# Every block its own leg, with scores, selection and attention as wide as its causal keys

## The chip, the cores and the metric

The kernel is one program on one NeuronCore of a Trainium2 chip. The metric is the device time of one execution in microseconds; the times shown are from three executions, and one more execution was profiled.

## What is computed

Two layers over 512 positions of width 1024. Each layer normalises its input, projects it once, and runs three mixers beside each other: a state-space group, a gMLP group and a sparse attention group with eight heads. Their outputs go through one output projection and are added to the input. Then follows the PEER part: each position picks 128 experts (8 heads of 16), and each expert is one row of 1024 numbers in the table peer_u and one in peer_v. The attention and the PEER part, cut to what matters here:

```python
topk = min(256, L // 4)                      # 128
key_chunk = jnp.arange(L) // CHUNK           # chunks of 64
...
    score = jnp.einsum('bth,bths->bts', wi, jax.nn.relu(s))
    adm = key_chunk[None, :] <= (qpos // CHUNK)[:, None]
    score = jnp.where(adm[None], score, -jnp.inf)
    sel_score, sel = lax.top_k(score, topk)
    valid = jnp.isfinite(sel_score)
    ...
    logits = logits - slopes[None, None, :, None] * dist[:, :, None, :]
    logits = jnp.where(valid[:, :, None, :], logits, -jnp.inf)
    probs = jax.nn.softmax(logits, axis=-1)
...
    act = jax.nn.gelu(jnp.einsum('tkd,td->tk', peer_u[e], hx))
    return jnp.einsum('tk,tkd->td', g * act, peer_v[e])
```

A query sees the keys of its own 64-position chunk and of those before it. Of a block of 128 queries, block b sees at most (b + 1) * 128 keys, and those of block 0 see at most 128, which is as many as the selection takes.

## The kernel before

The 512 positions are four blocks of 128. The program is a row of ten **legs**, and it is a software pipeline: leg (l, b) runs the mixers and the routing of block b in layer l, and beside them the PEER work of blocks before it. These go one leg behind (the dots with peer_u) and two legs behind (the mixing of peer_v). I write (0,0) to (1,3) for the eight legs with mixers; two tail legs without mixers follow. Leg (0,0) has no gathers at all, (0,1) has those of peer_u alone, and all later ones up to the first tail leg have both. The helper `legs` (L163) lists them, and legs 2 and 3 of each layer stand in the program once, as the body of a loop (`eng.Fori(2, NB)`).

The gathers: `fetch_u` and `fetch_v` on GpSimd (POOL, L231 and L238) each bring 128 rows, one per partition, 512 KB together, into one of the eight buffers of ringU or ringV. GpSimd works in program order: four U fetches, then four V fetches, 32 times a leg. Before a U fetch it waits until VectorE has made the dot that used the buffer (`S["dots"]`), before a V fetch until TensorE has mixed the buffer (`S["mixed"]`). A dot is one instruction on VectorE over 128x1024 (L709). A mixing step is 16 listed matmuls on TensorE over four buffers (L430), and 32 steps make a leg.

The order is written out by hand. VectorE and TensorE both run in program order, and the tables DOTS and MIX say how many dots (of 128) and mixing steps (of 32) are done by each stage of the mixers; DOTS_FIRST and MIX_FIRST hold for block 0 of a layer:

```python
"scored": 38, "picked": [38 + (r + 1) * 10 // 16 for r in range(16)],
"heads": [48 + (h + 1) * 26 // 8 for h in range(8)], "values": 82
...
"gated": 7, "picked": 11, "heads": [11, 12, 13, 13, 14, 15, 16, 17]
```

The attention part of a leg, by engine. TensorE makes the scores of four index heads (L578, into pw). ScalarE (ACT) takes their relu (L347). VectorE weighs and adds them (L1028, L1031), adds the mask `am`, and takes the top 128 in 16 rounds of MAX and MATCH_REPLACE over 512 columns (L1037, L1038), with dots between the rounds; what was replaced is the selection, and L1040 and L1041 make the penalty `D_` of it. Beside that TensorE makes mixing steps, and in block 0 of a layer also the last three of twelve modulation products (L461), and then the logits of the first two heads (L602).

For each head h then: VectorE adds `D_` to the logits (L1058) and takes the maximum (L1061); ScalarE takes the exponential (L372); VectorE scales the head before by the reciprocal sum (L1050, L1052), and makes three or four dots. TensorE transposes the probabilities in four pieces of 128 (L438), ScalarE copies them (L299), TensorE multiplies them with the cached keys in four pieces (L616), makes the logits of head h + 2, and where the table says so one mixing step. After the eighth head come the value projection (L627), the output projection (L636), the second norm, and the queries and routing. The next leg begins when all engines have met (`meet`, L155 on).

SyncE (SP) loads the weights through two buffers, in program order; in block 0 of a layer the load of norm2_g (L1251) waits for the first sum of the scores, `S["scored"]`.

## Time and profile before

| | |
|---|---|
| median of 3 runs | 3995.33 us (3994.73 to 3996.36) |
| the profiled execution | 3987.24 us, of it the span 3985.4 us |
| busy: VectorE, GpSimd, TensorE, ScalarE | 2473.5, 2298.0, 1942.4, 240.0 us |
| DMA | 1282.43 MB, 322 GB/s over the span |
| of the 16 DMA engines' span | 71.4% fetches of GpSimd, 13.7% the other large queue |

The span is the time from the first to the last instruction. The profiled execution is 8 us, or 0.2%, under the median of the three runs. An engine's busy time says how long it computed, not whether anyone waited for it: for that the timeline of a leg has to be read, with what ended each wait in brackets.

### The profile page before, as it was taken

How to read it: one execution, taken by the hardware profiler on the slowest of the kernel's cores; microseconds unless marked ns; L12 is line 12 of the kernel's file. 1: busy time of each engine (PE TensorE's matmuls, PEld its weight loads, DVE VectorE, ACT ScalarE, POOL GpSimd, SP SyncE). 2: the span in 40 equal slices, each digit the busy share in tenths (PEclk: the TensorE clock that was granted, in tenths of full speed). 3: DMA queues.
4: the chain of work that ended last, by engine and by line, in shares of the span. 5: the costliest groups of instructions: out<-in, count | busy, mean ns of one | idle time of the engine just before them, and what ended most of it. 6: DMA issues, size and time to landing. Idle time of an engine off the chain costs nothing. (4 is left out here: it accounts for less than half of the span.)

```text
span 3985.4 us, 30915 instructions
## 1 busy us (share of the span) xinstructions
PE 1942.4 (49%) x10338; PEld 984.3 (25%) x10338; DVE 2473.5 (62%) x5939; ACT 240.0 (6%) x539; POOL 2298.0 (58%) x2063
## 2 busy tenths in 40 slices
PE   7762351646344552676735363545526462233344
PEld 3542331413122220243314131322204130000000
DVE  4527878774768557567577746785577748544300
ACT  0110010001000100000100010001000000000000
POOL 0002455665767576456656657675766666777654
PEclk9876665767667675887767676666757685666667
DMA  7424777988989798999989889897989898999987
GB/s 236 140 75 154 236 251 256 346 342 325 408 308 390 281 402 313 333 410 378 350 306 368 343 320 399 318 395 273 402 311 373 297 373 350 368 409 409 350 303 272
DMA packets 417266, 1282.43 MB, mean 322 GB/s; under 512 B 52810, under 2 KB 63818, under 8 KB 417106
## 3 DMA queue, kind: packets, MB, share of 16 engines
q0 software_dynamic: 294912, 1073.87, 71.4%
q1 hardware_dynamic: 103252, 202.59, 13.7%
q10 hardware_dynamic: 18944, 3.96, 0.5%
q8 instruction: 87, 1.43, 0.1%
q14 instruction: 71, 0.58, 0.0%
HBM read 1271.89 MB, written 8.39 MB: 321 GB/s over the span
## 5 line engine op out<-in xcount | busy, mean ns | idle before, releaser
L709 DVE CUSTOM_DVE_ANT_0 ringU<-ringU,h2g 128x1024 f32<-128x1024 f32 x1024 | 1222.8, 1223 | 731.2 <-DMA ringU<-in_peer_u,idx_g 661.6
L238 POOL DMA_INDIRECT ringV<-in_peer_v,idxT x960 | 1050.7, 1094 | 731.0 <-PE py L430 469.4
L231 POOL DMA_INDIRECT ringU<-in_peer_u,idx_g x960 | 1101.6, 1147 | 499.4 <-issue 275.8
L430 PE MATMUL py<-ringV,wm 128*32 128x512 f32 x4096 | 771.2, 893 | 1071.4 <-DMA ringV<-in_peer_v,idxT 857.0
L430 PEld LDWEIGHTS py<-ringV,wm 128*32 128x32 f32 x4096 | 152.2, 143 | 1567.2 <-issue 1512.3
L496 PE MATMUL pj<-hT,wring 128*128 128x128 f32 (+1 forms) x2560 | 330.2, 295 | 51.2 <-DMA wring<-in_w_in 44.4
L496 PEld LDWEIGHTS pj<-hT,wring 128*128 128x128 f32 (+1 forms) x2560 | 321.0, 205 | 81.6 <-DMA wring<-in_w_in 53.6
L231 POOL DMA_INDIRECT ringU<-in_peer_u,idx_w x64 | 67.2, 1050 | 386.2 <-DVE gate_w L1156 357.6
L438 PE MATMUL pj<-ident,wk 128*128 128x128 f32 x264 | 63.3, 378 | 426.5 <-DVE wk L1052 365.4
L461 PE MATMUL pj<-wring,mixT 128*128 128x512 f32 x288 | 140.4, 644 | 70.8 <-DMA wring<-in_w_mod 66.7
L1175 DVE TENSOR_TENSOR wk<-py,g2g 128x1024 f32<-128x1024 f32 x8 | 9.8, 1224 | 265.6 <-PE py L430 263.7
L438 PEld LDWEIGHTS pj<-ident,wk 128*128 128x128 f32 x264 | 39.5, 185 | 495.2 <-DVE wk L1052 430.0
L616 PE MATMUL pw<-hT,ckv_all 128*128 128x128 f32 x512 | 121.6, 412 | 43.9 <-ACT hT L299 43.9
L616 PEld LDWEIGHTS pw<-hT,ckv_all 128*128 128x128 f32 x512 | 103.8, 301 | 65.9 <-ACT hT L299 65.9
L1058 DVE SCALAR_TENSOR_TENSOR wk<-wk,pw 128x512 f32<-128x512 f32 x64 | 43.8, 684 | 119.6 <-PE pw L602 119.3
L636 PE MATMUL pj<-wring,mixT 128*128 128x512 f32 x256 | 115.6, 610 | 1.4 <-ACT mixT L299 1.4
L238 POOL DMA_INDIRECT ringV<-in_peer_v,idxTn x64 | 74.6, 1165 | 51.5 <-PE py L430 34.4
L461 PEld LDWEIGHTS pj<-wring,mixT 128*128 128x128 f32 x288 | 57.9, 207 | 150.9 <-issue 123.3
L1037 DVE MAX8 top<-wk 128x8 f32<-128x512 f32 x128 | 88.6, 692 | 2.1
L438 PE MATMUL pj<-ident,hh 128*128 128x128 f32 x128 | 31.4, 427 | 119.6 <-DVE hh L926 119.6
L372 ACT ACTIVATE wk<-wk,cols 128x512 f32<-128x512 f32 x64 | 46.2, 722 | 704.8 <-DVE cols L1061 704.8
L1038 DVE MATCH_REPLACE8 wk<-top,wk 128x512 f32<-128x512 f32 x128 | 86.5, 675 | 0.0
(295 smaller groups left out, 2206.7 us busy)
## 6 DMA issues: line engine op xcount, KB each, us to landing
wring<-in_w_in SPq DMA_DIRECT2D x28, 2048.0 KB, 20.1
wring<-in_w_mod SPq DMA_DIRECT2D x24, 2048.0 KB, 10.1
wring<-in_w_out SPq DMA_DIRECT2D x16, 2048.0 KB, 20.3
wring<-in_peer_w_q SPq DMA_DIRECT2D x16, 2048.0 KB, 21.9
ringU<-in_peer_u,idx_g POOLq DMA_INDIRECT x960, 7.9
ringV<-in_peer_v,idxT POOLq DMA_INDIRECT x960, 7.3
wring<-in_w_in SPq DMA_DIRECT2D x8, 784.0 KB, 17.3
x_mix<-xs SPq DMA_DIRECT2D x8, 512.0 KB, 19.2
```

The costliest lines, as they stand in the source:

```text
L231: pool.indirect_dma_start(out=ringU[k % NR][:, :], out_offset=None, in_=ux, in_offset=bass.IndirectOffsetOnAxis(ap=idx[:, k:k + 1], axis=0 ...
L238: pool.indirect_dma_start(out=ringV[r % NR][:, :], out_offset=None, in_=vx, in_offset=bass.IndirectOffsetOnAxis(ap=idx[:, 32 * j + m:32 * ...
L372: a.activation(wk[:, 3072 + (h % 2) * 512:3584 + (h % 2) * 512], wk[:, 2048 + (h % 2) * 512:2560 + (h % 2) * 512], ACT.Exp, bias=col(NM + ...
L430: mm = t.matmul(py[32 * j:32 * j + 32, c * 512:(c + 1) * 512], wm[e % 2][:, at:at + 32], ringV[(4 * m + j) % NR][:, c * 512:(c + 1) * 512] ...
L438: m = t.transpose(dst, src, ident[:, :])
L461: t.matmul(pj[n % 2][:, :], crep[:, k * 128:(k + 1) * 128], wt[:, k * 512:(k + 1) * 512], start=k == 0, stop=False)
L496: mm = t.matmul(dst, wt[:, k * gc + c0:k * gc + c0 + width], hT[:, k * 128:(k + 1) * 128], start=k == 0, stop=k == KT - 1)
L616: mm = t.matmul(pw[:, 1024 + (h % 4) * 128:1152 + (h % 4) * 128], ckv_all[:, s * 128:(s + 1) * 128], hT[:, (h % 2) * 512 + s * 128:(h % 2) ...
L636: mm = t.matmul(pj[n][:, :], mixT[:, k * 128:(k + 1) * 128], wt[:, k * 512:(k + 1) * 512], start=k == 0, stop=k == KT - 1)
L709: v.tensor_tensor_reduce(out=ringU[k % NR][:, :], in0=ringU[k % NR][:, :], in1=h2g[:, :], scale=1.0, scalar=0.0, op0=ALU.mult, op1=ALU.add ...
L1037: link(v.max(top8[:, :], sc))
L1038: link(v.match_replace(sc, top8[:, :], sc, GONE))
```

## The change

It does four things. The loops are written out, so that b is a number in every leg. `seen(b)` gives W = (b + 1) * 128, and scores, relus, the sums, the selection's rounds, the eight heads' logits, maxima, exponentials and scalings are W columns wide in place of 512; transposes and products with the keys have b + 1 pieces in place of four. In block 0 the scores, relus, sums and all 16 rounds are left out, `D_` is made of the mask and the distance alone, and the dots that stood between the rounds (one after `scored` and so on) follow in one row. And norm2_g waits for the state-space product `y_ps` in place of `scored`. For b = 3 the width stays at 512. In the diff, hunks that only rename or simplify are left out.

```diff
@@ -64,7 +64,11 @@


 def is_first(b):
-    return isinstance(b, int) and b == 0
+    return b == 0
+
+
+def seen(b):
+    return (b + 1) * T


 def dots_by(b, stage, i=None):
...
@@ -164,11 +168,11 @@

             leg(0, 0, True, None, None)
             leg(0, 1, True, 0, None)
-            with eng.Fori(2, NB) as b:
+            for b in range(2, NB):
                 leg(0, b, True, (b - 1) * LANDU, (0, b - 2, (b - 2) * LANDV))
             leg(1, 0, True, 3 * LANDU, (0, 2, 2 * LANDV))
             leg(1, 1, True, 4 * LANDU, (0, 3, 3 * LANDV))
-            with eng.Fori(2, NB) as b:
+            for b in range(2, NB):
                 leg(1, b, True, (b + 3) * LANDU, (1, b - 2, (b + 2) * LANDV))
             leg(1, None, False, 7 * LANDU, (1, 2, 6 * LANDV))
             leg(1, None, False, None, (1, 3, 7 * LANDV))
...
@@ -342,9 +346,10 @@
                         a.activation(wk[:, 512 + j * 128:640 + j * 128], pj[0][:, 256 + j * 128:384 + j * 128], ACT.Tanh,
                                      scale=0.5, bias=col(BGH + j)).then_inc(S["z_th"], 1)

-                    for h in range(IH):
+                    W = seen(b)
+                    for h in range(IH if b > 0 else 0):
                         a.wait_ge(S["sc_ps"], h + 1)
-                        a.activation(wk[:, 2048 + h * 512:2560 + h * 512], pw[:, h * 512:(h + 1) * 512],
+                        a.activation(wk[:, 2048 + h * 512:2048 + h * 512 + W], pw[:, h * 512:h * 512 + W],
                                      ACT.Relu).then_inc(S["relu_sb"], 1)
                     for n in range(2):
                         a.wait_ge(S["qa_ps"], n + 1)
...
@@ -359,7 +364,7 @@
                         a.wait_ge(S["pt_ps"], h + 1)
                         if h >= 2:
                             a.wait_ge(S["o_ps"], h - 1)
-                        copy(hT[:, (h % 2) * 512:(h % 2 + 1) * 512], pj[h % 2][:, :], "pt_sb")
+                        copy(hT[:, (h % 2) * 512:(h % 2) * 512 + W], pj[h % 2][:, 0:W], "pt_sb")
                         if h in (3, 7):
                             a.wait_ge(S["o_ps"], h + 1)
                             if h == 3:
...
@@ -369,7 +374,8 @@
                         a.wait_ge(S["nmax"], h + 1)
                         if h >= 2:
                             a.wait_ge(S["pt_ps"], h - 1)
-                        a.activation(wk[:, 3072 + (h % 2) * 512:3584 + (h % 2) * 512], wk[:, 2048 + (h % 2) * 512:2560 + (h % 2) * 512],
+                        a.activation(wk[:, 3072 + (h % 2) * 512:3072 + (h % 2) * 512 + W],
+                                     wk[:, 2048 + (h % 2) * 512:2048 + (h % 2) * 512 + W],
                                      ACT.Exp, bias=col(NM + h), accum_out=col(DEN + h)).then_inc(S["exp_done"], 1)
                         if h >= 1:
                             evac_p(h - 1)
...
@@ -572,10 +578,11 @@
                     mm.then_inc(S["z_ps"], 1)

                     t.wait_ge(S["bu_used"], 1)
-                    for h in range(IH):
+                    W = seen(b)
+                    for h in range(IH if b > 0 else 0):
                         lo = 64 * (h % 2)
                         at = 1408 if h < 2 else 1536
-                        t.matmul(pw[:, h * 512:(h + 1) * 512], pr[lo:lo + 64, at:at + 128], kiT_all[lo:lo + 64, :],
+                        t.matmul(pw[:, h * 512:h * 512 + W], pr[lo:lo + 64, at:at + 128], kiT_all[lo:lo + 64, 0:W],
                                  start=True, stop=True).then_inc(S["sc_ps"], 1)

                     t.wait_ge(S["z_th"], 2)
...
@@ -592,29 +599,30 @@
                         modulation(MOD_EARLY, 12, hT)
                         t.wait_ge(S["mod_sb"], 12)
                     mix(mix_by(b, "picked"))
-                    t.wait_ge(S["relu_sb"], 4)
+                    if b > 0:
+                        t.wait_ge(S["relu_sb"], 4)
                     t.wait_ge(S["qa_sb"], 2)

                     def logits(h):
                         if h >= 2:
                             t.wait_ge(S["lg_used"], h - 1)
                         q = hh[:, (h % 2) * 512 + (h // 2) * 128:(h % 2) * 512 + (h // 2 + 1) * 128]
-                        t.matmul(pw[:, (h % 2) * 512:(h % 2 + 1) * 512], q, ckvT_all[:, :],
+                        t.matmul(pw[:, (h % 2) * 512:(h % 2) * 512 + W], q, ckvT_all[:, 0:W],
                                  start=True, stop=True).then_inc(S["lg_ps"], 1)

                     def values(h):
                         t.wait_ge(S["p_ready"], h + 1)
                         if h >= 2:
                             t.wait_ge(S["pt_sb"], h - 1)
-                        for s in range(4):
+                        for s in range(b + 1):
                             turn(pj[h % 2][:, s * 128:(s + 1) * 128], wk[:, 3072 + (h % 2) * 512 + s * 128:3200 + (h % 2) * 512 + s * 128],
-                                 "pt_ps" if s == 3 else None)
+                                 "pt_ps" if s == b else None)
                         t.wait_ge(S["pt_sb"], h + 1)
                         if h == 4:
                             t.wait_ge(S["o_sb"], 1)
-                        for s in range(4):
+                        for s in range(b + 1):
                             mm = t.matmul(pw[:, 1024 + (h % 4) * 128:1152 + (h % 4) * 128], ckv_all[:, s * 128:(s + 1) * 128],
-                                          hT[:, (h % 2) * 512 + s * 128:(h % 2) * 512 + (s + 1) * 128], start=s == 0, stop=s == 3)
+                                          hT[:, (h % 2) * 512 + s * 128:(h % 2) * 512 + (s + 1) * 128], start=s == 0, stop=s == b)
                         mm.then_inc(S["o_ps"], 1)
                     for h in range(AH):
                         logits(h)
...
@@ -1017,28 +1025,33 @@
                         v.tensor_copy(hT[:, :].rearrange("p (k m) -> p k m", k=KT), spread_c()).then_inc(S["crep_ready"], 1)

                     v.wait_ge(S["ckv_cached"], 2)
-                    sc, am, nd, D_ = wk[:, 0:512], wk[:, 1024:1536], wk[:, 1536:2048], wk[:, 512:1024]
+                    W = seen(b)
+                    sc, am, nd, D_ = wk[:, 0:W], wk[:, 1024:1024 + W], wk[:, 1536:1536 + W], wk[:, 512:512 + W]
                     note(v.tensor_scalar(col(WSC, 4), pr[:, 1792:1796], 1.0 / 16, None, ALU.mult))

-                    note(v.tensor_scalar(am, nd0[:, :], col(LIMP), NEG, ALU.is_ge, ALU.mult))
-                    note(v.tensor_scalar(nd, nd0[:, :], col(B128), None, ALU.subtract))
+                    note(v.tensor_scalar(am, nd0[:, 0:W], col(LIMP), NEG, ALU.is_ge, ALU.mult))
+                    note(v.tensor_scalar(nd, nd0[:, 0:W], col(B128), None, ALU.subtract))
                     settled()
                     link(v.scalar_tensor_tensor(nd, nd, -1.0, nd, ALU.mult, ALU.min))
-                    v.wait_ge(S["relu_sb"], 1)
-                    link(v.tensor_scalar(sc, wk[:, 2048:2560], col(WSC), None, ALU.mult))
-                    for h in range(1, IH):
-                        v.wait_ge(S["relu_sb"], h + 1)
-                        link(v.scalar_tensor_tensor(sc, wk[:, 2048 + h * 512:2560 + h * 512], col(WSC + h), sc, ALU.mult, ALU.add))
-                    v.tensor_tensor(sc, sc, am, ALU.add).then_inc(S["scored"], 1)
-                    v.wait_ge(S["scored"], 1)
-                    link(v.tensor_tensor(nd, am, nd, ALU.add))
-                    gathered(dots_by(b, "scored"))
-                    for r in range(TOPK // 8):
-                        link(v.max(top8[:, :], sc))
-                        link(v.match_replace(sc, top8[:, :], sc, GONE))
-                        gathered(dots_by(b, "picked", r))
-                    link(v.tensor_scalar(D_, sc, -2e38, NEG, ALU.is_gt, ALU.mult))
-                    link(v.tensor_tensor(D_, D_, nd, ALU.add))
+                    if b == 0:
+                        link(v.tensor_tensor(D_, am, nd, ALU.add))
+                        gathered(dots_by(b, "picked", TOPK // 8 - 1))
+                    else:
+                        v.wait_ge(S["relu_sb"], 1)
+                        link(v.tensor_scalar(sc, wk[:, 2048:2048 + W], col(WSC), None, ALU.mult))
+                        for h in range(1, IH):
+                            v.wait_ge(S["relu_sb"], h + 1)
+                            link(v.scalar_tensor_tensor(sc, wk[:, 2048 + h * 512:2048 + h * 512 + W], col(WSC + h), sc,
+                                                        ALU.mult, ALU.add))
+                        link(v.tensor_tensor(sc, sc, am, ALU.add))
+                        link(v.tensor_tensor(nd, am, nd, ALU.add))
+                        gathered(dots_by(b, "scored"))
+                        for r in range(TOPK // 8):
+                            link(v.max(top8[:, :], sc))
+                            link(v.match_replace(sc, top8[:, :], sc, GONE))
+                            gathered(dots_by(b, "picked", r))
+                        link(v.tensor_scalar(D_, sc, -2e38, NEG, ALU.is_gt, ALU.mult))
+                        link(v.tensor_tensor(D_, D_, nd, ALU.add))
                     if is_first(b):
                         v.wait_ge(S["mod_sb"], 10)
                         v.wait_ge(S["gain2_in"], 16)
...
@@ -1048,14 +1061,14 @@
                     def scale_p(h):
                         v.wait_ge(S["exp_done"], h + 1)
                         link(v.reciprocal(col(RD + h), col(DEN + h)))
-                        P = wk[:, 3072 + (h % 2) * 512:3584 + (h % 2) * 512]
+                        P = wk[:, 3072 + (h % 2) * 512:3072 + (h % 2) * 512 + W]
                         v.tensor_scalar(P, P, col(RD + h), None, ALU.mult).then_inc(S["p_ready"], 1)
                     for h in range(AH):
                         v.wait_ge(S["lg_ps"], h + 1)
                         if h >= 2:
                             v.wait_ge(S["exp_done"], h - 1)
-                        L = wk[:, 2048 + (h % 2) * 512:2560 + (h % 2) * 512]
-                        v.scalar_tensor_tensor(L, D_, 2.0 ** (-8.0 * (h + 1) / AH), pw[:, (h % 2) * 512:(h % 2 + 1) * 512],
+                        L = wk[:, 2048 + (h % 2) * 512:2048 + (h % 2) * 512 + W]
+                        v.scalar_tensor_tensor(L, D_, 2.0 ** (-8.0 * (h + 1) / AH), pw[:, (h % 2) * 512:(h % 2) * 512 + W],
                                                ALU.mult, ALU.add).then_inc(S["lg_used"], 1)
                         v.wait_ge(S["lg_used"], h + 1)
                         v.tensor_reduce(col(NM + h), L, AXX, ALU.max, negate=True).then_inc(S["nmax"], 1)
...
@@ -1247,7 +1260,7 @@
                     if is_first(b):
                         for n in range(MOD_EARLY, 12):
                             weights(A["w_mod"][l], n * 512, 512)
-                        sp.wait_ge(S["scored"], 1)
+                        sp.wait_ge(S["y_ps"], 1)
                         sp.dma_start(wk[:, 3 * D:4 * D], bcast(A["norm2_g"][l])).then_inc(S["gain2_in"], 16)
                     for name in ("w_out", "peer_w_q"):
                         for n in range(2):
```

On VectorE, the program of leg (0,0) from the copy for the modulation (hT) on. `nd` and `wk` hold distance, mask and scores, `pw` the logits. Before:

```order
L1017 COPY hT<-cols 128x1024
...
L1026 SCALAR_TENSOR_TENSOR wk<-wk 128x512
L1028 TENSOR_SCALAR wk<-wk,cols 128x512
L1031 SCALAR_TENSOR_TENSOR wk<-wk,cols 128x512 x3
L1032 TENSOR_TENSOR wk<-wk 128x512
L1034 TENSOR_TENSOR wk<-wk 128x512
L1037 MAX top<-wk 128x8
L1038 MATCH_REPLACE wk<-top,wk 128x512
...
L1041 TENSOR_TENSOR wk<-wk 128x512
L915 SCALAR_TENSOR_TENSOR modb<-modb,wk 128x1024
L1058 SCALAR_TENSOR_TENSOR wk<-wk,pw 128x512
```

And in the change:

```order
L1025 COPY hT<-cols 128x1024
L1030 TENSOR_SCALAR cols<-pr 128x4
L1032 TENSOR_SCALAR wk<-nd,cols 128x128
L1033 TENSOR_SCALAR wk<-nd,cols 128x128
L1035 SCALAR_TENSOR_TENSOR wk<-wk 128x128
L1037 TENSOR_TENSOR wk<-wk 128x128
L923 SCALAR_TENSOR_TENSOR modb<-modb,wk 128x1024
L1071 SCALAR_TENSOR_TENSOR wk<-wk,pw 128x128
L1074 TENSOR_REDUCE cols<-wk 128x1
```

The 16 rounds and the sums ahead of them are gone, and the first head follows the scaled modulation directly.

On TensorE, one head of leg (0,1): logits (pw from ckvT_all), transposes (pj from wk), product with the keys (pw from hT). Before:

```order
L602 MATMUL pw<-ckvT_all,hh 128x512 x2
L438 MATMUL pj<-ident,wk 128x128 x4
L616 MATMUL pw<-hT,ckv_all 128x128 x4
L602 MATMUL pw<-ckvT_all,hh 128x512
```

And in the change:

```order
L610 MATMUL pw<-ckvT_all,hh 128x256 x2
L444 MATMUL pj<-ident,wk 128x128 x2
L624 MATMUL pw<-hT,ckv_all 128x128 x2
L610 MATMUL pw<-ckvT_all,hh 128x256
```

The order of a head is the same, with half the pieces and half the width.

## Rows read from the trace of the kernel before

**Rows 1.** The page: a dot among the costliest groups (busy, mean ns); a U fetch among DMA issues (us to landing).

```profile
L709 DVE CUSTOM_DVE_ANT_0 ringU<-ringU,h2g 128x1024 f32<-128x1024 f32 x1024 | 1222.8, 1223 | 731.2 <-DMA ringU<-in_peer_u,idx_g 661.6
...
ringU<-in_peer_u,idx_g POOLq DMA_INDIRECT x960, 7.9
```

**Rows 2.** Windows by leg: stretch, length, busy (instructions), granted clock, DMA share, GB/s.

```profile
363.00:714.20 351.20, 130.69 (x723) 98.30 (x723) 289.81 (x680) 26.88 (x56) 181.76 (x139) 0.63 0.74 252
...
2107.70:2539.60 431.90, 211.27 (x1235) 111.37 (x1235) 292.21 (x677) 27.83 (x64) 286.08 (x252) 0.71 0.91 346
...
3424.80:3760.60 335.80, 114.19 (x521) 22.42 (x525) 165.81 (x282) 2.31 (x10) 245.85 (x250) 0.66 1.01 401
```

**Rows 3.** Timeline, VectorE, leg (0,0): start, length, instruction [idle before it].

```profile
172.01 0.48 DVE L1023 TENSOR_SCALAR wk<-nd,cols 128x512 f32<-128x512 f16 x1
...
202.72 0.69 DVE L1041 TENSOR_TENSOR wk<-wk 128x512 f32<-128x512 f32 x1
...
204.71 0.69 DVE L1058 SCALAR_TENSOR_TENSOR wk<-wk,pw 128x512 f32<-128x512 f32 x1
...
213.69 0.69 DVE L1058 SCALAR_TENSOR_TENSOR wk<-wk,pw 128x512 f32<-128x512 f32 x1 [5.68 <-PE pw L602]
...
221.37 0.69 DVE L1058 SCALAR_TENSOR_TENSOR wk<-wk,pw 128x512 f32<-128x512 f32 x1 [5.68 <-PE pw L602]
```

**Rows 4.** Timeline, TensorE, leg (0,0).

```profile
174.81 7.13 PE L461 MATMUL pj<-wring,hT 128*128 128x512 f32 x16 [0.83 <-ACT hh L351]
...
199.91 1.98 PE L602 MATMUL pw<-ckvT_all,hh 128*128 128x512 f32 x4 [0.69 <-ACT modb L299]
...
217.56 2.07 PE L616 MATMUL pw<-hT,ckv_all 128*128 128x128 f32 x8 [0.69 <-ACT hT L299]
...
260.81 14.00 PE L636 MATMUL pj<-wring,mixT 128*128 128x512 f32 x32 [0.70 <-ACT mixT L299]
```

**Rows 5.** Groups by line: instruction, shapes, count | busy us, mean ns | idle before.

```profile
L1037 DVE MAX8 top<-wk 128x8 f32<-128x512 f32 x128 | 88.6, 692 | 2.1
...
L1038 DVE MATCH_REPLACE8 wk<-top,wk 128x512 f32<-128x512 f32 x128 | 86.5, 675 | 0.0
...
L1111 DVE MAX8 pr<-wk 128x8 f32<-128x256 f32 x64 | 21.7, 411 | 0.3
...
L1115 DVE MATCH_REPLACE8 wk<-pr,wk 128x256 f32<-128x256 f32 x64 | 26.1, 408 | 0.0
...
L1003 DVE SCALAR_TENSOR_TENSOR wk<-pr,cols,pj 128x128 f32<-128x128 f32 x16 | 4.8, 339 | 0.0
```

**Rows 6.** Timeline, VectorE, leg (0,1).

```profile
505.47 0.69 DVE L1058 SCALAR_TENSOR_TENSOR wk<-wk,pw 128x512 f32<-128x512 f32 x1
...
560.69 0.49 DVE L1052 TENSOR_SCALAR wk<-wk,cols 128x512 f32<-128x512 f32 x1
```

**Rows 7.** Who waited, GpSimd: 2254 to 2350 us, then 1880 to 1953 us: total, times, longest.

```profile
POOL ringV L238 <- PE py L430: 27.7, 4, 12.2
...
POOL ringV L238 <- PE py L430: 14.8, 4, 7.0
```

**Rows 8.** Timeline, leg (1,1), then two mixing steps of leg (1,0).

```profile
2265.38 2.71 PE L430 MATMUL py<-ringV,wm 128*32 128x512 f32 x16
2268.35 0.93 POOL L238 DMA_INDIRECT ringV<-in_peer_v,idxT  x1 [11.40 <-PE py L430]
...
1857.67 1.92 PE L430 MATMUL py<-ringV,wm 128*32 128x512 f32 x16
1869.15 3.64 PE L430 MATMUL py<-ringV,wm 128*32 128x512 f32 x16 [9.56 <-DMA ringV<-in_peer_v,idxT]
```

**Rows 9.** Timeline, VectorE, where legs (0,3), (1,1) and (1,3) begin.

```profile
1152.83 1.23 DVE L709 CUSTOM_DVE_ANT_0 ringU<-ringU,h2g 128x1024 f32<-128x1024 f32 x1 [10.88 <-DMA ringU<-in_peer_u,idx_w]
...
2104.52 1.22 DVE L709 CUSTOM_DVE_ANT_0 ringU<-ringU,h2g 128x1024 f32<-128x1024 f32 x1 [0.74 <-DVEq L161]
...
2985.06 1.23 DVE L709 CUSTOM_DVE_ANT_0 ringU<-ringU,h2g 128x1024 f32<-128x1024 f32 x1 [7.21 <-issue]
```

4 lines of the change are left out of this document (2 added, 2 removed).

## The prediction

> **What bounds the kernel now.** I first cut the span into its ten legs and read for each the DMA share, to see which legs have slack there. In the first tail leg there is nothing but gathers, and it shows the pace that they can reach: 256 fetches in 335.8 us, 1.31 us each, at 401 GB/s [rows 2]. Leg (1,1), with mixers and both rings, takes 431.9 us at 346 GB/s, and leg (0,1), with the U ring alone, 351.2 us at 252 GB/s [rows 2]. So no leg with mixers is bound by DMA throughout; each has places where the fetches stand still. Shorter mixers can only win there.
>
> The second view is who waited, for GpSimd, in the attention stage of a leg. In leg (1,1) GpSimd waits 27.7 us for TensorE's mixing between 2254 and 2350 us, in four waits, and in leg (1,0) 14.8 us between 1880 and 1953 us [rows 7]. The longest is in rows 8: the mixing step at 2265.38 stands in TensorE's program behind the first head, which waits for the end of the selection, and the V fetch at 2268.35 comes after 11.40 us of idleness. The change works on exactly this stage.
>
> The third view is the timeline of the legs (0,0) and (0,1), where the ring is absent or fed in time. There the chain VectorE, ScalarE, TensorE itself is the time: in leg (0,0) head follows head every 221.37 − 213.69 = 7.68 us, 5.68 of them idle on VectorE [rows 3].
>
> **Leg (0,0): 33 us.** Sums and selection go: on VectorE all from 172.01 to the end of L1041 at 203.4 [rows 3], 31.4 us, except four short instructions. But they have a cover that stays. TensorE makes its three modulation products from 174.81 on and ends in the logits at 199.91, and these wait for ScalarE's copy of the modulation [rows 4]. With four score products and their relus gone, TensorE comes to this about 1.8 us earlier (its program has nothing else ahead), so the first head can start at 198.6 in place of 204.71 [rows 3]: of the 31 us only 6 count. The load of norm2_g sits behind the last modulation weights in SP's program, so its new condition moves nothing, and the gain (L915) fits under the modulation.
>
> The heads are the larger term. Of the 7.68 us of a cycle, everything scales with the width: a 128-column instruction of VectorE takes 0.34 us where 512 columns take 0.69 [rows 3, 5], and TensorE has one piece where L616 takes 2.07 us for four [rows 4]. My estimate for the new cycle is 3.0 us: VectorE 1.1 (four instructions), transpose 0.45, copy 0.3, product 0.45, logits 0.45, and four handovers of 0.05. The first head's scaling comes about 1.6 us behind the first head's start, at 200.2, and seven cycles later it is 221. With the last product, two copies and the value projection the output projection, 260.81 before [rows 4], starts at 226 to 228. I take 33 us, between 30 and 35.
>
> **Leg (0,1), W = 256: 27 us.** No mixing here, and VectorE is the bound. A round costs 692 + 675 ns at 512 columns and 411 + 408 at 256 [rows 5]: 16 x 0.548 = 8.8 us. Ten other instructions of the mask, the sums and `D_` save about 0.27 each, as 0.69 falls to 0.41 [rows 3, 5], 2.8 in all. From 505.47 to 561.18 (the last scaling) the heads take 55.7 us [rows 6]. They hold 26 dots of 1.19 us (1222.8 us of busy time over 1024, rows 1), 31 us, and eight times four instructions of 2.0 us together, 16, so some 9 us are waits. Now the four cost 1.3 us, 41.4 in all, and with 0.6 us of waits 42, saving 13.7. The waits nearly go, since TensorE's part of a head (the 5.68 us of idleness in rows 3) falls to about 3.6, which three or four dots cover. Behind the last head 1.6 us of TensorE's chain go too. Sum 26.9. The U fetches keep up: 26 dots in 42 us, one in 1.6, against 1.31 a fetch.
>
> **Legs with both rings.** Here the fetches decide, so I count what the longest waits of GpSimd lose.
> - (1,1), W = 256: VectorE would end the selection 11.6 us earlier. But the dots behind it need U fetches that GpSimd issued without a pause up to 2257, and these land 7.9 us after their issue [rows 1], so the second head's first instruction comes only some 5 us earlier; with shorter transposes, copy and product the mixing step comes 6.8 us earlier. Of the other long wait (12.2 us, rows 7) the part behind the landed dot (10.4 us, with 3.3 of mixing) loses 2.3, the two short waits 2, the end of the heads 1.6. Sum 13.
> - (0,2) and (1,2), W = 384: by the same count 5 + 1.1 + 1 + 0.8 = 8 each.
> - (1,0), W = 128: the logits wait for the mixing step at 1869.15, whose V rows landed late [rows 8]. Only the 1.8 us of scores ahead of the modulation move it. The first head starts at about 1871.5 in place of 1879.9: 8. The heads then are bound by 42 fetches (18 dots and six mixing steps), 42 x 1.31 = 55 us, plus the rest of the waits of rows 7, against 70: 7. Sum 15.
> - (0,3) and (1,3): nothing. The two tail legs: nothing.
>
> The bounds: below, these four legs give nothing, because TensorE and VectorE only wait longer for the same fetches; above, the waits of rows 7 go fully with the instruction time: 28 for (1,1), 20 for each of (0,2) and (1,2), 28 for (1,0).
>
> **The loops.** Leg (1,3) begins at the loop's jump back. VectorE's first dot comes there after 7.21 us of idleness that no wait explains, where leg (1,1), written out, begins after 0.74 [rows 9]. Some of that is the landing of the first U rows in any case, so I take 4 us for this seam, and 0 for (0,3), whose first dot waits 10.88 us for its rows anyway. Bounds 0 and 14 (twice 7).
> The Trainium skill, Runtime: NRT & Kernel Launch, section Instruction fetch mechanics, says that prefetch is sequential and that a taken branch to a page not held stalls until it is fetched. By it alone both jumps back would be worth the 7 us, and the sum 10 us more.
>
> **The sum.** 33 + 27 + 8 + 0 + 15 + 13 + 8 + 0 + 4 = 108 us. The profiled execution took 3987.24 us, of it the span 3985.4; it would take 3879. It lies 8 us under the median of the runs shown, so against that I forecast 3995 − 108 = 3887 us.
>
> **The rivals.**
> - **The fetches take it all.** In the four legs with both rings and W below 512 the gain is nothing: what is saved in the attention stage comes back as waiting in the same stage. For it: selection is under fetches without a pause. Against it: 27.7 us of GpSimd's waits are for TensorE [rows 7]. Gain 33 + 27 = 60, or 3935 us. Chance 0.2.
> - **The waits for mixing go altogether.** Then the upper bounds hold: 33 + 27 + 28 + 2 x 20 + 28 + 7 = 163, or 3832 us. For it: the stage moves far less than 401 GB/s. Against it: most of a fetch group's way (10 us of issue, 8 of landing) does not know W. Chance 0.15.
> - **TensorE falls to its lower clock: slower.** The same mixing step takes 1.92 us at one place and 3.64 at another [rows 8]; these are the two levels, 2.4 and 1.2 GHz, and the slow one came after 9.56 us of idleness. Narrower heads leave TensorE idler between steps. If all 27 mixing steps in the attention of the four legs ran slow, 1.72 us each, that is 46 us; if the output projection (14.00 us in leg (0,0), rows 4) ran at half speed in five legs, 70 more. Together 116 us against 108: 4003 us. It decides only if nearly all of these now run at 2.4 GHz and none does afterwards, and many already run slow. Chance 0.02. The Trainium skill, TensorE: Matmul & The Clock Gate, section HAM oscillation — how this bites in real kernels, says that groups of matmuls shorter than the waits between them start slow each time, which speaks against this change; the trace agrees that it happens, at the step after the 9.56 us.
> - **It does not do what it says:** the listing of the program shows the widths, so this is left at 0.01 (no change).
>
> **How the numbers follow.** The forecast has 0.62. Its own range: 30 to 35, 24 to 28, twice 3 to 12, 8 to 22, 6 to 20, 0 to 14 give 74 to 143, or 3852 to 3921. The first rival at 3935 must be inside, and about half of the second. So 3840 to 3938. Two tenths of a percent, 8 us, is about what a measurement of this kernel can tell. All but the last two cases are faster by more: 0.97, 0.01, 0.02.
>
> **What would show it.** In leg (0,0) the first head at 198 to 199 us, directly after TensorE's logits, heads 3 us apart, and the output projection at 226 to 228. In leg (0,1) rounds of 0.82 us and a length of 324. In (1,1) the wait of 11.40 us near 4 to 5, and a length near 419; (0,3) and (1,3) within 3 us of before. It is wrong if heads in (0,0) stay above 4 us apart, or if (1,1) keeps 27 us of GpSimd's waits for mixing.

## The result, and the profile after

The changed kernel took 3903.05 us (median of 4 runs, 3899.09 to 3912.6) against 3995.16 us for the kernel before, a ratio of 0.9772 with a 95% interval of 0.9754 to 0.9791: 92 us less. The forecast was 3887 us with 3840 to 3938 as its range. The profiled execution took 3899.09 us, 88 less than that of before, where the sum had 108.

These are lines of the page of the changed kernel: busy times, then two of the groups, with the idle time before them and its main cause.

```profile
PE 1857.6 (48%) x10034; PEld 932.4 (24%) x10034; DVE 2355.1 (60%) x5829; ACT 213.7 (5%) x531; POOL 2302.5 (59%) x2063
...
L717 DVE CUSTOM_DVE_ANT_0 ringU<-ringU,h2g 128x1024 f32<-128x1024 f32 x1024 | 1226.3, 1224 | 813.3 <-DMA ringU<-in_peer_u,idx_g 749.7
L242 POOL DMA_INDIRECT ringV<-in_peer_v,idxT x960 | 1058.5, 1103 | 699.0 <-PE py L436 435.9
```

VectorE has 118 us less to do and waits 88 us longer for U rows: 749.7 where it waited 661.6 [rows 1]. The windows of the same three legs as in [rows 2] (stretch, length, busy, granted clock, DMA share, GB/s):

```profile
333.30:659.90 326.60, 118.96 (x675) 92.72 (x675) 273.88 (x680) 22.83 (x56) 184.60 (x139) 0.60 0.79 271
2042.40:2464.50 422.10, 201.11 (x1187) 102.34 (x1187) 274.30 (x673) 23.75 (x64) 284.68 (x249) 0.68 0.93 351
3337.10:3672.70 335.60, 111.23 (x525) 22.56 (x529) 165.86 (x282) 2.31 (x10) 245.33 (x250) 0.66 1.01 402
```

The length of each leg, from one load of `xs` to the next, in the profiled executions. The column "again" is run `e5_change`, on a chip where the kernel before took 3997 us. Its gains are counted from the same profile of before.

| leg | before | change | again | forecast | gained |
|---|---|---|---|---|---|
| (0,0) | 356.1 | 326.4 | 328.6 | 33 | 30, 28 |
| (0,1) | 351.2 | 326.6 | 326.9 | 27 | 25, 24 |
| (0,2) | 431.3 | 431.6 | 428.1 | 8 | 0, 3 |
| (0,3) | 437.2 | 435.1 | 436.8 | 0 | 2, 0 |
| (1,0) | 525.0 | 515.9 | 515.1 | 15 | 9, 10 |
| (1,1) | 431.8 | 422.0 | 422.1 | 13 | 10, 10 |
| (1,2) | 442.7 | 435.5 | 433.9 | 8 | 7, 9 |
| (1,3) | 442.5 | 437.2 | 440.4 | 0 and 4 (seam) | 5, 2 |
| tails | 560.5 | 560.2 | 557.8 | 0 | 0, 3 |

These are lengths from one profile each, and a leg whose program two runs share differs between them by up to 7 us: (0,0) took 328.6 us in e5 and 324.5 in e6, (1,1) 427.5 in e3 and 431.7 in e4, (1,3) 446.3 and 453.5 in the same two. On the chip of e1 to e4, wide to narrow (e1 to e4), the legs (0,2), (1,0), (1,1) and (1,2) gained 7, 14, 7 and -1 us. So how a gain splits over the legs with both rings is known to some 5 us a leg only; the four together gained 26 and 32 us by the table and 27 there.

**Leg (0,0).** First VectorE's timeline of the changed kernel (start, length, instruction, idle before), to be set against [rows 3]; then TensorE's, for [rows 4].

```profile
195.16 1.22 DVE L923 SCALAR_TENSOR_TENSOR modb<-modb,wk 128x1024 f32<-128x1024 f32 x1 [21.74 <-DMA wk<-in_norm_g]
...
203.31 0.29 DVE L1071 SCALAR_TENSOR_TENSOR wk<-wk,pw 128x128 f32<-128x128 f32 x1 [6.93 <-PE pw L610]
...
210.12 0.29 DVE L1071 SCALAR_TENSOR_TENSOR wk<-wk,pw 128x128 f32<-128x128 f32 x1 [2.15 <-PE pw L610]
...
213.28 0.29 DVE L1071 SCALAR_TENSOR_TENSOR wk<-wk,pw 128x128 f32<-128x128 f32 x1 [2.15 <-PE pw L610]
```

```profile
171.01 3.06 PE L593 MATMUL pj<-pr,wuk 64*128 64x128 f32 x16 [0.76 <-issue]
...
174.76 8.95 PE L467 MATMUL pj<-wring,hT 128*128 128x512 f32 x16 [0.69 <-ACT hh L356]
...
184.70 7.13 PE L467 MATMUL pj<-wring,hT 128*128 128x512 f32 x16
...
193.84 7.13 PE L467 MATMUL pj<-wring,hT 128*128 128x512 f32 x16 [0.96 <-DMA wring<-in_w_mod]
...
202.72 0.71 PE L610 MATMUL pw<-ckvT_all,hh 128*128 128x128 f32 x4 [0.69 <-ACT modb L303]
...
230.15 15.43 PE L644 MATMUL pj<-wring,mixT 128*128 128x512 f32 x32 [0.70 <-ACT mixT L303]
```

Heads now follow each other every 3.16 us, not 7.68. But the first one comes only 1.4 us earlier than before (204.71 [rows 3]) and not 6, since TensorE is later at its logits, 202.72 against 199.91 [rows 4]. Its first modulation product takes 8.95 us where it took 7.13.

**Leg (1,1).** VectorE's timeline of the changed kernel, with the mask, the end of the selection, and the first and the last of eight heads; then who waited in the heads' stretch, VectorE of before (2254.7 to 2328 us) and VectorE of the changed kernel (2183.4 to 2257.2 us).

```profile
2142.97 0.35 DVE L1032 TENSOR_SCALAR wk<-nd,cols 128x256 f32<-128x256 f16 x1
...
2182.68 0.29 DVE L1053 TENSOR_SCALAR wk<-wk 128x256 f32<-128x256 f32 x1
...
2183.46 0.42 DVE L1071 SCALAR_TENSOR_TENSOR wk<-wk,pw 128x256 f32<-128x256 f32 x1
...
2256.70 0.42 DVE L1071 SCALAR_TENSOR_TENSOR wk<-wk,pw 128x256 f32<-128x256 f32 x1
```

```profile
DVE ringU L709 <- DMA ringU<-in_peer_u,idx_g: 23.7, 4, 9.1
```

```profile
DVE ringU L717 <- DMA ringU<-in_peer_u,idx_g: 34.8, 9, 8.9
```

From the mask to the first head it is 40.5 us. Before it was 47.5, by the same two lines:

```profile
2207.28 0.48 DVE L1023 TENSOR_SCALAR wk<-nd,cols 128x512 f32<-128x512 f16 x1
...
2254.76 0.69 DVE L1058 SCALAR_TENSOR_TENSOR wk<-wk,pw 128x512 f32<-128x512 f32 x1
```

From the first head to the last it is 73.2 us, and was 72.5. So behind the narrow selection the narrow heads, 2.0 us of VectorE's work each brought down to 1.3, shortened nothing in their own stretch: VectorE waits there 11 us longer for rows.

GpSimd's two long waits of [rows 7, 8] in the changed kernel, again the V fetches that follow the mixing steps behind the first heads:

```profile
2199.72 0.93 POOL L242 DMA_INDIRECT ringV<-in_peer_v,idxT  x1 [0.32 <-PE py L436]
...
2232.00 0.93 POOL L242 DMA_INDIRECT ringV<-in_peer_v,idxT  x1 [9.77 <-PE py L436]
```

The wait of 11.40 us is gone altogether: GpSimd issues without a pause from the selection into the heads. Counted from the mask, the mixing step that it waited for ends 4.3 us earlier (at 56.5 us, before 60.8), and GpSimd comes to this fetch 6.7 us later (56.4, before 49.7). For it had become slower at issuing. The 40 fetches ahead of this one, from 2200.76 and from 2136.87 us on, took 56.2 us before and 62.5 in the changed kernel. Where the added time sits can be read off row by row, on VectorE and on GpSimd of the changed kernel:

```profile
2181.53 1.23 DVE L717 CUSTOM_DVE_ANT_0 ringU<-ringU,h2g 128x1024 f32<-128x1024 f32 x1
```

```profile
2181.74 1.82 POOL L235 DMA_INDIRECT ringU<-in_peer_u,idx_g  x1 [0.30 <-issue]
2183.87 0.94 POOL L235 DMA_INDIRECT ringU<-in_peer_u,idx_g  x1 [0.30 <-issue]
```

An issue that begins while VectorE makes a dot ends 0.88 us after the dot (2182.68, when VectorE's next instruction starts); the others mostly take 0.94 us. From 650 to 3300 us of the changed kernel 464 issues begin under a dot, and eight in ten of them end 0.86 to 0.89 us after it; before, it is the same with 470, from 700 to 3400 us. With the selection narrow the dots between its rounds follow each other faster, and 19 of the 40 issues begin under one, where 15 did. They are longer than 0.94 us by 12.9 us together, and were by 6.0.

### The profile page after: what moved, and what is told of

Same layout as the page of the kernel before. It is cut to its first block and busy times, and to the rows that moved or that the text cites. A ratio compares the mean times of both kernels' runs of the same rounds, so it can differ in the third digit from the quotient of the medians.

```text
span 3897.3 us, 29946 instructions
## 1 busy us (share of the span) xinstructions
PE 1857.6 (48%) x10034; PEld 932.4 (24%) x10034; DVE 2355.1 (60%) x5829; ACT 213.7 (5%) x531; POOL 2302.5 (59%) x2063
## 5 line engine op out<-in xcount | busy, mean ns | idle before, releaser
L717 DVE CUSTOM_DVE_ANT_0 ringU<-ringU,h2g 128x1024 f32<-128x1024 f32 x1024 | 1226.3, 1224 | 813.3 <-DMA ringU<-in_peer_u,idx_g 749.7
L502 PE MATMUL pj<-hT,wring 128*128 128x128 f32 (+1 forms) x2560 | 328.4, 295 | 50.9 <-DMA wring<-in_w_in 43.9
L502 PEld LDWEIGHTS pj<-hT,wring 128*128 128x128 f32 (+1 forms) x2560 | 319.4, 204 | 80.7 <-DMA wring<-in_w_in 54.0
L444 PE MATMUL pj<-ident,wk 128*128 128x128 f32 x168 | 49.1, 403 | 407.0 <-DVE wk L1065 337.8
L467 PE MATMUL pj<-wring,mixT 128*128 128x512 f32 x288 | 140.5, 645 | 71.9 <-DMA wring<-in_w_mod 68.5
L444 PEld LDWEIGHTS pj<-ident,wk 128*128 128x128 f32 x168 | 25.5, 189 | 453.4 <-DVE wk L1065 379.8
L624 PE MATMUL pw<-hT,ckv_all 128*128 128x128 f32 x320 | 83.7, 420 | 33.7 <-ACT hT L303 33.7
L717 DVE DVE_READ_ACCUMULATOR2_ANT acts<- 128x1 f32 x1024 | 83.3, 81 | 0.0
L624 PEld LDWEIGHTS pw<-hT,ckv_all 128*128 128x128 f32 x320 | 66.1, 295 | 55.5 <-ACT hT L303 55.5
L377 ACT ACTIVATE wk<-wk,cols 128x128 f32<-128x128 f32 (+3 forms) x64 | 36.0, 562 | 636.4 <-DVE cols L1074 636.4
L1071 DVE SCALAR_TENSOR_TENSOR wk<-wk,pw 128x128 f32<-128x128 f32 (+3 forms) x64 | 31.0, 484 | 59.0 <-PE pw L610 58.7
```

The source lines that it names most:

```text
L377: a.activation(wk[:, 3072 + (h % 2) * 512:3072 + (h % 2) * 512 + W], wk[:, 2048 + (h % 2) * 512:2048 + (h % 2) * 512 + W], ACT.Exp, bias=c ...
L444: m = t.transpose(dst, src, ident[:, :])
L467: t.matmul(pj[n % 2][:, :], crep[:, k * 128:(k + 1) * 128], wt[:, k * 512:(k + 1) * 512], start=k == 0, stop=False)
L502: mm = t.matmul(dst, wt[:, k * gc + c0:k * gc + c0 + width], hT[:, k * 128:(k + 1) * 128], start=k == 0, stop=k == KT - 1)
L624: mm = t.matmul(pw[:, 1024 + (h % 4) * 128:1152 + (h % 4) * 128], ckv_all[:, s * 128:(s + 1) * 128], hT[:, (h % 2) * 512 + s * 128:(h % 2) ...
L717: v.tensor_tensor_reduce(out=ringU[k % NR][:, :], in0=ringU[k % NR][:, :], in1=h2g[:, :], scale=1.0, scalar=0.0, op0=ALU.mult, op1=ALU.add ...
```

## The experiments

Five kinds of question: the loops, the parts of the change, TensorE's clock in leg (0,0), what the legs with two rings wait for, and whether there is a better version. Runs e1 to e4 shared one chip, e5 to e8 a second, and e9 to e11 were timed together at another time, on the chip of e1 to e4. The kernel before took 4080, 3997 and 4083 us there, so ratios are compared, or times that were taken together.

**e1, the loops written out and nothing else.** In the kernel before:

```diff
-            with eng.Fori(2, NB) as b:
+            for b in range(2, NB):
```

(twice)

> The kernel before with its loops written out and nothing else changed (all widths 512, all rounds kept). Theory of the prediction: only the seam at the jump back into leg (1,3) shortens, by 4 us, so 3991 us, and legs (0,2), (0,3), (1,2) keep their 431, 437 and 443 us. Rival (both jumps back cost what the row of the second showed): 7 us at each, 3981 us. Rival (register values in the loop's waits cost nothing, the idle 7 us is the landing of the rows anyway): 3995 us.

Measured 4082.28 us, ratio 1.000 (0.9979 to 1.0021). No gain can be seen; more than 9 us for both jumps together is excluded. At the place something is: these are the first two dots of leg (1,3) in VectorE's timeline of e1.

```profile
3031.69 1.23 DVE L709 CUSTOM_DVE_ANT_0 ringU<-ringU,h2g 128x1024 f32<-128x1024 f32 x1 [2.77 <-DMA ringU<-in_peer_u,idx_w]
...
3035.98 1.23 DVE L709 CUSTOM_DVE_ANT_0 ringU<-ringU,h2g 128x1024 f32<-128x1024 f32 x1 [2.34 <-DMA ringU<-in_peer_u,idx_w]
```

The idleness of 7.21 us with no releaser [rows 9] has become a wait of 2.77 us for the first row, 4.4 us less. But the second dot waits another 2.34 us for its own row, where before it followed at 2987.04, 1.98 us after the first, so 2 us of the 4.4 are left at the second dot. Before, the third then came after 1.67 us of idleness that again has no releaser; in e1 it follows at once, and 3.9 us are left there. What remains of them at the leg's end is below what the run can resolve. In the changed kernel the first dot's wait is 3.35 us, likewise for its row.

**e2, block 0 alone.** The change, but blocks 1 to 3 work on 512 columns:

```diff
 def seen(b):
-    return (b + 1) * T
+    return T if b == 0 else SEQ
```

> The change with block 0 alone narrow and without selection; blocks 1 to 3 are 512 wide again. Reading of the changed profile: legs (0,0) and (1,0) give 30 and 9 us, the written-out legs about 5, so some 3951 us, and legs (0,1) and (1,1) go back to 351 and 432 us. Rival (the legs with both rings are bound by their fetches, and what (1,0) and (1,1) won is only another phase of the same stream): leg (1,0) keeps 525 us, 3960 us.

Measured 4031.02 us, ratio 0.9892 (0.9863 to 0.992): 49 of the 86 us that the change gives on this chip (e4, below) are block 0's. In leg (0,0) 326.3 us against 355.2 in e1, in (1,0) 527.6 against 542.7, so (1,0) gave 15 us here; the rival, which had it keep its length, is out.

**e3, block 2 wide again.** The change with `seen(2)` at 512.

> The change with block 2 at 512 columns again (blocks 0 and 1 stay narrow). The prediction's term was 8 us for each of legs (0,2) and (1,2), so it would have this 16 us above the change. The changed profile shows leg (0,2) no shorter and (1,2) 7 us shorter, part of which could be the missing loop. Theory now: the selection is under fetches without a pause, so 384 columns are worth 0 to 4 us together and this is within 4 us of the change. Rival: 16 us slower than the change.

Measured 4004.98 us, 0.9813 (0.9787 to 0.9839). Against e2, block 1 is worth 26 us by medians; its legs went from 353.9 to 331.5 and from 436.9 to 427.5 us. Against e4, the whole width table, block 2 is worth 11, 7.5 of it in leg (0,2) and 4.0 in (1,2). Six runs of each spread over 24 and 32 us, so the difference is uncertain by about 13 us, and neither the expected 0 to 4 nor the rival's 16 is excluded.

**e4, the scores of block 0 kept on TensorE, unread.** In the change:

```diff
-                    for h in range(IH if b > 0 else 0):
+                    WS = SEQ if b == 0 else W
+                    for h in range(IH):
...
-                        t.matmul(pw[:, h * 512:h * 512 + W], ..., kiT_all[lo:lo + 64, 0:W],
+                        t.matmul(pw[:, h * 512:h * 512 + WS], ..., kiT_all[lo:lo + 64, 0:WS],
```

> The change with the four score products of block 0 issued on TensorE at 512 columns as before; nobody reads them, and relus, sums and selection stay out. Theory: leaving them out let TensorE fall to its lower clock before the products with wuk and the first modulation product (3.06 and 8.95 us in place of 1.60 and 7.13), so with them back the logits of leg (0,0) come at 199 to 200 us in place of 202.7, and the whole is 2 to 4 us faster than the change. Rival (the modulation weights came late and would again): logits at 202 us or later, and the time is equal or up to 2 us longer.

Measured 3994.17 us, 0.9779 (0.9751 to 0.9807): as a whole, the change. The place shows what was asked, in TensorE's timeline of this run:

```profile
170.07 2.75 PE L586 MATMUL pw<-kiT_all,pr 64*128 64x512 f32 x8
172.66 1.60 PE L594 MATMUL pj<-pr,wuk 64*128 64x128 f32 x16
174.95 7.13 PE L467 MATMUL pj<-wring,hT 128*128 128x512 f32 x16 [0.69 <-ACT hh L356]
...
200.05 0.71 PE L611 MATMUL pw<-ckvT_all,hh 128*128 128x128 f32 x4 [0.69 <-ACT modb L303]
...
227.64 16.69 PE L645 MATMUL pj<-wring,mixT 128*128 128x512 f32 x32 [0.70 <-ACT mixT L303]
```

Four matmuls whose result nobody reads bring the 16 small ones from 3.06 back to 1.60 us and the product behind them from 8.95 to 7.13, and the logits start at 200.05 (in e2, same chip, without them: 202.64). The granted clock from 170 to 200 us is 0.97, where it was 0.98 before and 0.86 in the changed kernel. The last product no longer waits for its weights either. But 28 us later the output projection takes 16.69 us (e2: 15.40), the next product (L502) 17.02 (e2: 16.39), and the leg is 325.8 us long, e2's 326.3: of 2.5 us, 1.9 are given back in these two.

**e5, the change on the chip of the next three.**

> The change itself, timed on the same chip as the three that follow, so that they can be set against it. Both theories: about 0.977 of the kernel before, as on the first chip, and a first tail leg of the same length as before. Leg (1,1) about 10 us and leg (0,1) about 25 us shorter than before.

3901.72 us, 0.9768 (0.975 to 0.9786).

**e6, selection wide, heads narrow.** In the change, for blocks 1 and 2 the score matmuls, the relus and VectorE's selection at 512 columns; after the selection

```diff
-                    W = seen(b)
+                    W = 512 if b > 0 else T
                     sc, am, nd, D_ = wk[:, 0:W], wk[:, 1024:1024 + W], wk[:, 1536:1536 + W], wk[:, 512:512 + W]
...
+                    W = seen(b)
+                    D_ = wk[:, 512:512 + W]
```

> The change, but in blocks 1 and 2 the index scores, their relu and the whole selection work on 512 columns again; attention stays as narrow as the change made it. Theory A, in the legs with two rings only the narrow selection paid, because the heads there start 10 us apart whatever their width (they wait for rows): leg (1,1) goes back by all of its 10 us, (1,2) and (0,2) by what they gained (7 and 0), and leg (0,1), which has one ring, by about 11 of its 25 us; the whole is 27 to 30 us longer than the change, ratio to the kernel before about 0.984. Theory B, the heads were worth something there too: (1,1) and (1,2) keep at least half of what they gained, and the whole is 15 to 20 us longer than the change, about 0.981.

3919.77 us, 0.9815 (0.9797 to 0.9832), 18 us over e5, uncertain by about 8: the time of theory B. The legs: (0,1) 337.1 us, 10.2 longer than e5; (1,1) 424.2, 2.1 longer; (1,2) 440.0, 6.1 longer; (0,2) 431.7, 3.6 longer. So in leg (1,1) narrow heads alone keep 8 of the 10 us, but in (1,2) less than half, 3 of 9, which theory B had not; with legs known to some 5 us, neither can be leaned on alone. The place in (1,1) says more. Behind a wide selection the narrow heads take 67.5 us from the first to the last, where both narrow took 71.8 (e5) and both wide 72.5 (before), and the V fetch behind the first head still waits 8.93 us (e5: 1.39). So the heads do save, about 5 us, when the selection saves nothing. The opposite half, a narrow selection with wide heads, was not run.

**e7, the table of mixing steps one ahead.** In the change:

```diff
-MIX = {"start": 1, "projected": [2, 3, 4, 5], "states": 6, "gated": 7, "picked": 11,
-       "heads": [11, 12, 13, 13, 14, 15, 16, 17], "values": 18, "x1": 19, "h2": 20, "queries": [21, 22], "routing": 27}
+MIX = {"start": 1, "projected": [2, 3, 4, 5], "states": 6, "gated": 7, "picked": 12,
+       "heads": [12, 13, 14, 15, 15, 16, 17, 18], "values": 19, "x1": 20, "h2": 21, "queries": [22, 23], "routing": 28}
```

> The change, with the table of mixing steps advanced by one from the picked stage to the routing stage (legs of blocks 1 to 3 that have a V ring: five of them). Theory A, after the change the legs with two rings are held by GpSimd waiting for mixing steps that are tied to the heads, so that the next U rows are asked for late: GpSimd's 12 us wait at picked and heads shrinks, and each such leg is 3 to 10 us shorter, 15 to 50 us in all. Theory B, the transfers themselves are what is left: GpSimd waits less, VectorE waits for rows as long as before, and the time is that of the change within 0.3%.

The fourth head moves by two steps, all others by one.

3811.13 us, 0.9532 (0.9514 to 0.955), 91 us under the change: theory A in kind, at nearly twice its upper bound. Legs (0,2), (0,3), (1,2) and (1,3) are 17 to 21 us shorter than in e5, (1,1) 11. Who waited, GpSimd, leg (1,1): e5 from its first head on (2182.9 to 2300 us), then e7 in a stretch of the same length (2151 to 2268 us).

```profile
POOL ringV L242 <- PE py L436: 19.2, 5, 8.8
```

```profile
POOL ringV L242 <- PE py L436: 2.3, 5, 1.0
```

VectorE in the same two stretches:

```profile
DVE ringU L717 <- DMA ringU<-in_peer_u,idx_g: 58.0, 13, 9.4
DVE wk L1071 <- PE pw L610: 2.4, 1, 2.4
```

```profile
DVE ringU L717 <- DMA ringU<-in_peer_u,idx_g: 33.8, 11, 5.2
DVE wk L1071 <- PE pw L610: 12.9, 4, 7.3
```

The V fetches stand in GpSimd's program between the U fetches. A V fetch that waits for a mixing step holds up the U fetches behind it, and those VectorE. The table tied the mixing steps to the heads, and lagged one behind the dots: at the end of the heads 74 dots are done, 18.5 times four, and mixing stood at step 17. One ahead, TensorE waits 14.1 us for V rows in this stretch (none in e5) and VectorE 12.9 us for its logits, but VectorE waits 24 us less for U rows. Over the whole span GpSimd's waits for mixing fall from 469.5 to 357.0 us, and VectorE's for U rows from 750.5 to 605.2. The stretch shown is the heads alone; what the later entries of the table (values to routing) give was not separated.

**e8, the last spread of weights ahead of ScalarE's wait.**

```diff
                     columns(mix_by(b, "routing"))
+                    if not is_first(b):
+                        columns(28)
                     a.wait_ge(S["top_ready"], 1)
```

> The change, with ScalarE's last spread of the weights (the one that mixing steps 28 to 31 need) put ahead of its wait for the end of routing, in legs of blocks 1 to 3. Today TensorE waits for it 25.5 us in each such leg. Theory A, this wait keeps the last V rows and with them the end of the leg back: 3 to 10 us less per leg, 15 to 50 us in all. Theory B, it lies beside VectorE's routing, which ends later anyway: the wait disappears and the time is that of the change within 0.2%.

3856.16 us, 0.9649 (0.9631 to 0.9668), 46 us under e5. Who waited, TensorE, whole span, e5 and then e8:

```profile
PE py L436 <- ACT wm L296: 206.8, 12, 25.7
```

```profile
PE py L438 <- ACT wm L296: 80.5, 7, 16.8
```

The five legs that the edit touches are 6 to 11 us shorter than in e5, though the engine waited for is busy 5% of the time. The sum of these is 41 of the 46 us. Theory A.

**e9, the kernel before with e7's table.**

> The kernel before, with nothing but the table of mixing steps advanced by one. The change with that table took 3811 us, the change alone 3902, before 3997. Theory A, the table is worth the same whatever the width of the selection and of the heads (GpSimd's holes are set by the table alone): 3997 - 91 = 3906 us, ratio 0.977. Theory B, the change's time in legs with two rings came back as waits for rows because of this table, so that only with narrow selection and heads is there something to win: the table alone gives 30 to 60 us, about 3950 us, ratio 0.985 to 0.993, and the change on top of the table is worth 140 us rather than 95.

3994.68 us, 0.9797 (0.9772 to 0.9823), 88 us less than before on that chip. Nearer to theory A. The table is worth about the same with wide selection and heads as with narrow ones, 0.020 of the time against 0.024, so it explains at most a small part of why the change gave less than the sum. Both alone multiply to 0.9768 x 0.9797 = 0.957; e7 measured 0.9532 on another chip. Whether the two help each other by these 0.4% stays open.

**e10, the change with both.**

> The change with the advanced table and with ScalarE's last spread put ahead of its wait. Alone they gave 91 and 46 us. They sit at different places (heads; routing), so if each only closes its own hole they add: 3902 - 137 = 3765 us, 0.942. If both buy the same time, that of the rows fetched at the leg's end: 3800 us, 0.951.

3885.37 us, 0.9529 (0.9508 to 0.9551). That is the second expectation, both buying the same time. Set against e7's 0.9532, which was not timed together with it, the spread adds nothing that can be seen once the table is ahead; up to some 12 us could hide in the two intervals. e7, e8 and e10 all beat both kernels, and e7 is the simpler of the two fastest. e10 against e9 holds the narrow blocks and the spread together: 109 us, 30 in each of (0,0) and (0,1), 3 in (0,2), 12 in (1,1), but also 9 in (0,3), whose width did not change. So it doesn't tell what the narrow blocks alone give under that table.

**e11, further ahead.** e10 with `"states": 7, "gated": 8`, heads `[13, 14, 14, 15, 16, 17, 17, 18]`, values 20, x1 21, h2 22, queries `[23, 24]`.

> As the run with both, and the table a further step ahead at the states, gated and values to queries stages and at half of the heads. If GpSimd's wait for mixing still holds the rows there (5.0 and 6.7 us at the head of leg (1,1) with the advanced table): another 10 to 40 us. If TensorE now waits for V rows before it has done what VectorE needs, the heads get later: the same or up to 30 us longer than with both.

3976.36 us, 0.9749 (0.9728 to 0.977): 91 us over e10, three times the loss that was expected at most. Who waited, over the whole span: GpSimd for dots, then VectorE for TensorE's routing scores.

```profile
POOL ringU L235 <- DVE acts L719: 412.8, 64, 23.4
```

```profile
DVE pr L1100 <- PE pw L666: 175.3, 8, 33.1
```

In e10 these waits are 270.7 and 75.8 us. TensorE's own waits for V rows grew from 855.2 to 1106.6 us: mixing ahead of the dots puts V rows that have not come in front of TensorE's mixer work. The step of e7 pays, and this one, further ahead, costs as much as that had given. Which of its entries costs most was not tried.

## Why the prediction was right, and where it was not

The direction and the order of size came out by the forecast's own mechanism: a gain in (0,0) and (0,1) near what the instructions give, and less where two rings are fetched. The whole is 16 us above the forecast, well inside the range. Its signs of being wrong did not come: heads in (0,0) are 3.16 us apart, and in the 96 us from the first head of (1,1) GpSimd waits 14.2 us for mixing, not 27.7. The first rival (fetches take all, 60 us) is out, as (1,0), (1,1) and (1,2) together gave 26 and 28 us in the two profiles; so is the second (163 us). The third, TensorE at its lower clock, holds in a small part, below.

- **Leg (0,0), 33 us; 30 and 28.** The cycle of a head was right: 3.16 against 3.0. Wrong was the step "TensorE comes to this about 1.8 us earlier (its program has nothing else ahead)". It came 2.8 us later. Without the score matmuls TensorE was at its lower clock when it began the small products (3.06 in place of 1.60 us) and part of the first big one (8.95 in place of 7.13), and the last product then waited 0.96 us for weights. e4 put the matmuls back and with them the two durations, and the logits at 200.05. The first head came 4.7 us later than forecast (203.31, not 198.6), the output projection 2 to 4 (230.15), and it took 15.43 us in place of 14.00.
- **Leg (0,1), 27 us; 25 and 24.** Selection shrank by 11.0 us (11.6 with its ten small instructions) and the heads from 55.7 to 41.5, by 14.2 (13.7). The whole fell short as the mask comes 2.6 us later in the leg (97.5 us after the load of `xs`, against 94.9), which the sum did not hold; why it does was not looked into.
- **Leg (1,1), 13 us; 10.** Right in kind. The 11.6 us that selection saves became 7, as it ran into waits for rows (3.7 us, none before). "Of the other long wait the part behind the landed dot loses 2.3" gives 9.9 us, and it is 9.77. The failed step is the first term, which took the wait of 11.40 us down to 4 or 5: it is 0.32, and then the heads gave nothing in their stretch (73.2 against 72.5 us). The term held GpSimd's issuing fixed and let only the mixing step move, by 6.8 us. The step moved by 4.3, and the other 6.7 us of the lost wait are GpSimd coming later, 6.3 of them because its issues stretched under the denser dots. The same shows in every profile: with block 1's selection at 512 columns the 40 issues took 55.4 to 56.7 us (before, e1, e2, e6), at 256 columns 59.6 to 62.5 (the changed kernel, e3, e4, e5). So a shorter wait of GpSimd is a gain only as far as its issues did not grow. Its waits for mixing in 117 us from the first head on fell by 17 us, from 36.8 to 20.0; less the 6.3 us by which the 40 issues grew that is 10.5, and the leg gave 10:

```profile
POOL ringV L238 <- PE py L430: 36.8, 6, 12.2
```

```profile
POOL ringV L242 <- PE py L436: 20.0, 5, 9.8
```

- **(0,2) and (1,2), 8 each; 0 to 3 and 7 to 9.** The same count for two legs of the same width; by the table, in (0,2) it was 5 to 8 us too much. On the chip of e1 to e4 it is the other way round, 7 us in (0,2) and -1 to 4 in (1,2), so the miss of 8 us in one leg is not established, only that the two gave 6 to 12 us together in place of 16. In the profile of the table, in (0,2) the selection stretch lost 5.0 us (47.6 to 42.6) and the heads 1.0 (71.9 to 70.9), as counted, and nearly all of it was gone by the end of the leg. That the rest of the leg waits for rows is what the profile suggests; no run separates it.
- **(1,0), 15; 9 and 10.** On the chip of e1 to e4 it was 14 and 15 (e4 and e2 against e1), so the sum of 15 stands or is 6 us too much. Its two parts were both mis-sized, in opposite directions, which is luck. The first head comes 2.8 us earlier in the leg, not 8 (294.4 us after the load of `xs`, before 297.2), for it leaned on the same 1.8 us of TensorE's as leg (0,0). And the heads, from the first to the last, shrank by 14.1 us (57.5 to 43.4; in e1 and e2 60.0 and 43.2), not 7; they do not run at the pace of 42 fetches, 55 us.
- **The seam, 4; 2 to 5 in leg (1,3).** At the place the step was right at the first dot: 7.21 us of idleness became 2.77 in e1 and 3.35 in the changed kernel, in both the landing of the first rows. For the time of the whole e1 gives 1.000 (0.9979 to 1.0021), so 4 us can neither be shown nor denied. The Trainium skill (Runtime: NRT & Kernel Launch, section Instruction fetch mechanics) says that a taken branch to a page not held stalls; with the 7.21 us of the row at both jumps that would be an estimate of 14 us. The trace agrees that VectorE stands idle at the jump, but 14 us lie beyond e1's interval. That the rest lies beside the landing of rows is what the 2.77 us in e1 suggest.
- **The clock.** TensorE's lower clock showed at two places: 1.5 + 1.8 us in leg (0,0), and in the heads of leg (1,1), where the five mixing steps of the stretch took 13.9 us before (2.71, 1.92, 3.30, 3.30, 2.70) and 15.5 now (3.46, 3.04, 3.64, 1.92, 3.45). The Trainium skill (TensorE: Matmul & The Clock Gate, section HAM oscillation — how this bites in real kernels) says that groups of matmuls shorter than the waits between them start slow each time; the trace agrees in leg (1,1), where the steps behind waits of 16.93 and 9.87 us took 3.46 and 3.45 us and the one behind 1.45 us took 1.92. Many had been slow already, which is the rival's own condition for staying small.

The error of the sum, 108 against 88, is 3 and 2 us in the first two legs, 3 in (1,1), 8 in (0,2), 6 in (1,0) and 1 in (1,2), less 4 for the small gains where none was counted. By leg this is loose by some 5 us, but most of it lies in legs with both rings, the four of which with narrow widths gave 26, 32 and 27 us of the 44 in three pairs of profiles. There each saved microsecond was priced by the waits that it shortens, and GpSimd's own pace moved as well.

## What to carry to other kernels

Where a fetching engine takes its work in one order and waits in it for a consumer, first see which consumer it waits for and by what the consumer's turn is set: a table that let mixing lag one step behind the dots held 88 to 91 us, as much as all the removed arithmetic. Price removed work by leg: on a chain that nothing feeds it was worth nearly its full length, in the legs beside two fetch streams six to seven tenths of what was counted. When work goes from the engine that consumes the rows, look at the issuing engine's own durations as well as at its waits: they can grow as the consumer gets denser. Matmuls that are removed ahead of a dense stretch also take away what had raised TensorE's clock, so price the next product from a row at the lower level.
